# Routing of a mixture of experts: tile by tile under the output projection, in one block with the experts

## The chip, the cores and the metric

The kernel runs on one core of a Trainium2 chip. The metric is the device time of the whole program in microseconds (us); the time before is 2671.8 us, the median of three runs (2670.0 to 2675.88).

## What is computed

A trunk of two layers works on x, 1024 tokens of 1024 elements in float32. Each layer is an attention mixer with an output projection, a normalisation, a hierarchical mixture of experts, and a second normalisation:

```python
for layer in range(2):
    mix = ab_mixer(x, ...) if layer == 0 else c_mixer(x, ...)   # attention; ends with y @ w_out
    x = layer_norm(ALPHA * x + mix, ln_gain[layer, 0], ln_bias[layer, 0])
    ffn = hier_moe(x, ...)
    x = layer_norm(ALPHA * x + ffn, ln_gain[layer, 1], ln_bias[layer, 1])
```

The routing in hier_moe takes for each token the best of 4 groups by 4 group logits, and the best two of that group's 8 experts by 32 expert logits. The pairs (token, expert), 2048 of them, are then sorted by expert into blocks of 128 rows; every expert has one first block, and an expert with over 128 pairs has further ones. Each block is gathered, goes through the expert's gate, up and down matrices (1024x512, 1024x512, 512x1024), and its rows are added back with the weights of the pairs.

## The kernel before

Work is put into phases, each a block of its own with a program for every engine and a barrier at its end. For each layer: `attention`, `mixer_out`, `route`, `Moe.run`, `combine`. A float32 matrix is split in two float32r parts, a high part (ScalarE's copy, line 325 or 1574) and the rest (a subtraction, line 329, most of the time on VectorE), and a product is three matmuls in place of one.

`mixer_out` computes y @ w_out for 8 tiles of 128 tokens. Tiles 0 and 1 are computed chunk by chunk while y and w_out are being split. After that each tile is 48 matmuls of 512 columns (line 994): 24 for its first half of the columns, then the transposes of the normalised rows of the tile two before it (`router`, line 320), the other 24, and the logits of that earlier tile (`route_logits`, line 987). VectorE adds the product to the residual rows (line 1057), takes mean and variance (882 to 885); ScalarE takes the root and applies the norm (890, 902); VectorE multiplies by the gain (906); GpSimd adds the bias (910). SyncE stores the rows to DRAM, and ScalarE copies the transposed rows out of PSUM for the logits (1038), which VectorE keeps (1067). Two tiles are still to be transposed and given logits when the last product is done.

`route` starts when all logits are there. VectorE works on all 8 tiles at once in a chain of small operations (lines 1143 to 1232), each of which waits for the one before it: choice of group and experts, ranks of the pairs within their expert (TensorE adds them up, lines 1249 and 1250), number of further blocks, and one-hot rows from which TensorE makes the lists of rows of all 47 blocks (32 first blocks and up to 15 further ones; line 1253). Meanwhile SyncE loads up and down of expert 0, ScalarE splits expert 0's gate matrix and GpSimd makes its low part, and then SyncE loads the gate matrix of expert 1.

`Moe.run` clears two buffers for rows (line 1443), copies a list's column (1428), gathers rows with an indirect DMA on GpSimd (1431), and transposes them (320); ScalarE and VectorE split them, and the gate, up (1368) and down (1379) products follow. Experts are run in a loop, two in an iteration. Each of the three matrices has one raw buffer, refilled once VectorE has made its low part (1304). Results go to DRAM with an indirect DMA (1437). After 32 experts every engine reads the number of further blocks (`extra_blocks`) and runs these, if any; with these inputs there are none. SyncE fetches rows of x1 for `combine` (1272) once the last matrices have been split. `combine` then starts with loads of expert rows (1698) and adds each tile's two rows (1725, 1747, 1750) ahead of the second norm.

## Time and profile before

| | us |
|---|---|
| median of three runs | 2671.8 |
| the profiled execution's own time | 2675.71 |
| its span (first to last instruction) | 2673.9 |
| TensorE busy | 2286.0 |
| VectorE busy | 1812.6 |
| ScalarE busy | 1420.5 |
| GpSimd busy | 581.5 |

The mean granted clock of TensorE is 0.926 of full speed (2.4 GHz). Output projection and routing of the first layer lie between about 434 and 602 us of the span, those of the second between about 1795 and 1964; the experts follow to about 1222 and 2584. Times are read from the span's start; a busy time is a sum over instructions, and one of an engine which nothing waits for costs nothing.

### The profile page before, as it was taken

What the parts mean: (1) busy time and instruction counts of PE and PEld (TensorE: products, weight loads), DVE (VectorE), ACT (ScalarE), POOL (GpSimd) and SP (SyncE); (2) the same over time, 40 slices, a digit from 0 to 9 for tenths busy, and PEclk for the clock granted to TensorE, in tenths of its full rate; (3) what the DMA queues carried; (4) which work ended last, traced back from release to release, by engine and by line L of the source; (5) the groups of instructions that cost most, each with busy time, mean ns of one, the idle gap of its engine ahead of it and who ended that gap; (6) DMA issues with size and microseconds to landing.
All of it is one profiled execution on the core that took longest, in us unless ns stands there. A gap on an engine that the chain in (4) does not pass through costs nothing. (4 is left out here: it accounts for less than half of the span.)

```text
span 2673.9 us, 35450 instructions
## 1 busy us (share of the span) xinstructions
PE 2286.0 (85%) x12564; PEld 1862.1 (70%) x12564; DVE 1812.6 (68%) x2399; ACT 1420.5 (53%) x1705; POOL 581.5 (22%) x448
## 2 busy tenths in 40 slices
PE   7999997936999999992599999979649999999950
PEld 5767876835888887881478788868538888888840
DVE  3565556366888898885645455554458988889848
ACT  2454444215777777772344444442227777777732
POOL 0002332122232222322400000001212233232216
PEclk9999998958999999996699999999769999999985
DMA  3110012325999999996211111023329999999953
GB/s 111 29 29 28 29 32 82 111 110 214 369 367 367 373 369 367 372 353 231 75 42 38 39 35 43 27 66 111 145 91 366 377 379 379 372 370 360 361 221 144
DMA packets 125138, 533.52 MB, mean 200 GB/s; under 512 B 35904, under 2 KB 75864, under 8 KB 98408
## 3 DMA queue, kind: packets, MB, share of 16 engines
q1 hardware_dynamic: 102096, 496.86, 49.7%
q0 software_dynamic: 18432, 33.60, 3.4%
q10 hardware_dynamic: 4504, 1.66, 0.3%
q8 instruction: 66, 1.08, 0.2%
q14 instruction: 40, 0.33, 0.0%
HBM read 515.21 MB, written 50.39 MB: 212 GB/s over the span
## 5 line engine op out<-in xcount | busy, mean ns | idle before, releaser
L329 DVE TENSOR_TENSOR arena<-arena,arena 128x2048 fp32r<-128x2048 f32 (+1 forms) x454 | 946.4, 2119 | 98.6 <-ACT arena L1574 80.5
L1574 ACT CAST arena<-arena 128x2048 fp32r<-128x2048 f32 x380 | 705.0, 1918 | 183.6 <-PE psum L1368 103.8
L1368 PE MATMUL psum<-arena,arena 128*128 128x512 f32 x3072 | 737.2, 396 | 8.1 <-DVE arena L329 8.1
L1368 PEld LDWEIGHTS psum<-arena,arena 128*128 128x128 f32 x3072 | 571.8, 190 | 124.0 <-issue 5.6
L551 PE MATMUL psum<-arena,arena 128*128 128x512 f32 x2016 | 510.7, 405 | 5.9 <-ACT arena L659 5.8
L551 PEld LDWEIGHTS psum<-arena,arena 128*128 128x128 f32 x2016 | 375.2, 192 | 100.7 <-issue 11.6
L1379 PE MATMUL psum<-arena,arena 128*128 128x512 f32 x1536 | 367.6, 396 | 9.5 <-DVE arena L329 9.4
L1379 PEld LDWEIGHTS psum<-arena,arena 128*128 128x128 f32 x1536 | 288.4, 190 | 83.6 <-DVE arena L329 24.0
L320 PE MATMUL psum<-ident,arena 128*128 128x128 f32 x1024 | 160.4, 301 | 154.1 <-POOL arena L910 73.3
L329 DVE TENSOR_TENSOR arena<-psum,arena 128x512 fp32r<-128x512 f32 (+1 forms) x186 | 161.3, 873 | 172.8 <-ACT arena L1589 67.0
L320 PEld LDWEIGHTS psum<-ident,arena 128*128 128x128 f32 x1024 | 148.0, 198 | 181.0 <-POOL arena L910 82.9
L688 ACT ACTIVATE arena<-arena,arena 128x640 f32<-128x640 f32 (+4 forms) x192 | 120.0, 626 | 194.7 <-DVE arena L772 148.7
L1428 POOL COPY arena<-slot_rows 128x1 int32 (+1 forms) x64 | 62.9, 983 | 604.7 <-DMA expert_rows<-arena,arena 554.9
L994 PE MATMUL psum<-arena,arena 128*128 128x512 f32 x768 | 183.2, 396 | 8.1 <-ACT arena L325 6.3
L641 ACT COPY arena<-psum 128x512 f32<-128x512 f32 (+3 forms) x288 | 120.0, 466 | 129.9 <-PE psum L582 129.7
L994 PEld LDWEIGHTS psum<-arena,arena 128*128 128x128 f32 x768 | 143.6, 190 | 38.6 <-issue 6.8
L1431 POOL DMA_INDIRECT arena<-x_rows,arena x64 | 144.6, 2259 | 54.8 <-POOL arena L1428 53.1
L910 POOL TENSOR_TENSOR arena<-arena,arena 128x1024 f32<-128x1024 f32 x32 | 85.8, 2681 | 313.2 <-DVE arena L906 312.0
L582 PE MATMUL psum<-ident,arena 128*128 128x128 f32 x888 | 132.5, 280 | 23.2 <-POOL arena L876 9.2
L582 PEld LDWEIGHTS psum<-ident,arena 128*128 128x128 f32 x888 | 107.5, 143 | 52.2 <-POOL arena L876 12.1
L604 PE MATMUL psum<-arena,arena 128*64 128x128 f32 x1776 | 129.4, 287 | 0.0
L772 DVE CUSTOM_DVE_ANT_0 arena<-psum,arena 128x640 f32<-128x640 f32 (+3 forms) x192 | 104.9, 572 | 35.2 <-PE psum L570 34.5
(143 smaller groups left out, 1910.6 us busy)
## 6 DMA issues: line engine op xcount, KB each, us to landing
arena<-in_moe_w_gate SPq DMA_DIRECT2D x64, 2048.0 KB, 10.7
arena<-in_moe_w_up SPq DMA_DIRECT2D x64, 2048.0 KB, 8.6
arena<-in_moe_w_down SPq DMA_DIRECT2D x64, 2048.0 KB, 8.8
arena<-expert_rows SPq DMA_DIRECT2D x16, 1024.0 KB, 13.0
x_rows<-arena SPq DMA_DIRECT2D x24, 512.0 KB, 2.8
arena<-x_rows SPq DMA_DIRECT2D x24, 512.0 KB, 6.5
arena<-in_c_w_in SPq DMA_DIRECT2D x24, 512.0 KB, 4.1
arena<-in_x SPq DMA_DIRECT2D x16, 512.0 KB, 7.2
```

The costliest lines, as they stand in the source:

```text
L320: m = pe.transpose(dst_bank[:, j * P:(j + 1) * P], rows[:, c0 + j:rows.shape[1]:stride], ident[:])
L329: return eng.tensor_tensor(tile, src, high.bitcast(F32), ALU.subtract)
L551: mm = pe.matmul(job_bank(i, g), w[:, c * P:(c + 1) * P], xs[:, c, half_cols(g)], start=(a == 0), stop=(a == 23))
L582: mm = pe.transpose(bank(B_TURN + h)[:, (b - 4 * g) * P:(b - 4 * g + 1) * P], probs_of(s, h)[:, b * P:(b + 1) * P], ident[:])
L604: mm = pe.matmul(bank(B_OUT)[DH * h:DH * (h + 1), (t % 4) * P:(t % 4 + 1) * P], v_r[pair.kv][:, (kt + b) * P + DH * h:(kt + b) * P + DH * ...
L641: copy(probs_t[s % 2][h][:, a:b], bank(B_TURN + h)[:, 0:b - a]).then_inc(t_copied[h], 1)
L688: act.activation(probs_a[s % 2][h][:, 0:ahead + nk], biased[h][:, 0:ahead + nk], ACT.Exp, bias=low[s % 2][h], scale=-1.0, accum_out=rowsum ...
L994: return pe.matmul(bank(2 * (t % 2) + half), ys[:, c, t * P:(t + 1) * P], w[:, c, half * BANK:(half + 1) * BANK], start=(k == 0 and c == 0 ...
L1368: mm = pe.matmul(bank(o), cs[:, c * P:(c + 1) * P], ws[:, c * FF:(c + 1) * FF], start=(k == 0 and c == 0), stop=(k == 2 and c == CH - 1))
L1379: mm = pe.matmul(bank(B_Y + s), hs[:, c * P:(c + 1) * P], ws[:, c * D + s * BANK:c * D + (s + 1) * BANK], start=(k == 0 and c == 0), stop= ...
L1431: pool.indirect_dma_start(out=rows[b], out_offset=None, in_=x1_dram, in_offset=bass.IndirectOffsetOnAxis(ap=token[b], axis=0), bounds_chec ...
L1574: act.copy(w_hi[w][:, cols], self.raw[w][:, cols]).then_inc(hi_ready[w], 1)
```

## The change

`mixer_out` and `route` become a class `MixerOut`, whose parts are called from the engines' programs in `Moe.run`, so that projection, routing and experts of a layer are one block with no barrier inside. The norm is rearranged: GpSimd and ScalarE's long operation are out of it, and VectorE does subtraction of the mean with the gain, and the scaling with the bias. A tile's transposes and logits come one tile after its product in place of two. Routing is done in four groups of tiles (0 to 2, 3 to 5, 6, 7): `choose` picks experts, `ranks` (TensorE) adds up how many pairs precede, `select` makes one-hot rows, `lists` (TensorE) adds them into the lists of the first 32 blocks. The first groups are done between the norms of later tiles. What concerns further blocks is made later: `plan_extras` in the last step but one of the experts, `mark_extras` in the last, `list_extras` and `keep_extras` behind it, and all engines wait for `extras_ready` ahead of `extra_blocks`. Gain and bias are loaded after the residual rows, into the place of former weight buffers. Up and down of expert 0 are fetched when the last product is done, the low part of its gate matrix is made by VectorE after the lists are ready, and the gate matrix of expert 1 is fetched after that.

```diff
+AT_ROUTE, AT_CHOICE = 172.25, 201
+ARENA_KB = 202.75
...
+ROUTE_GROUPS = ((0, 1, 2), (3, 4, 5), (6,), (7,))
...
+                    sp.wait_ge(wl_ready, 6)
+                    for k, src in enumerate((ln_gain, ln_bias)):
+                        sp.dma_start(gain_bias[:, k, :], src[layer, 0:1, :].to_broadcast([P, D])
+                                     ).then_inc(gain_in, 16)
+                    sp.wait_ge(wl_ready, CH)
+                    moe.fetch(sp, 0, 0)
+                    for t in range(T):
+                        sp.wait_ge(normed, t + 1)
+                        sp.dma_start(x1_dram[t * P:(t + 1) * P, :], rows_all[:, t, :]).then_inc(x1_out, 16)
+                    sp.wait_ge(mix_ready, T)
...
+                    def ranks(g):
+                        pe.wait_ge(chosen_sent, g + 1)
+                        if g > 0:
+                            pe.wait_ge(added, T)
+                        for i, t in enumerate(ROUTE_GROUPS[g]):
+                            cols = rank_bank(g)[:, i * E:(i + 1) * E]
+                            mm = pe.matmul(cols, before_bf[:], chosen[:, t, :], start=True, stop=(t == 0))
+                            if t > 0:
+                                mm = pe.matmul(cols, ones_bf[:], so_far[:, t, :], start=False, stop=True)
+                        mm.then_inc(rank_ready, 1)
+                    def lists(g):
+                        for i in range(2 * len(ROUTE_GROUPS[g])):
+                            f = ENTRY[g] + i
+                            pe.wait_ge(ones_sent, f + 1)
+                            mm = pe.matmul(bank(B_LIST)[:, 0:E], at_slot[:, i, :], at_block[:, i, :],
+                                           start=(f == 0), stop=(f == ENTRIES - 1), skip_group_check=True)
+                        mm.then_inc(list_done, 1)
...
+                    for t in range(2, T):
+                        turned = 0 if t == 2 else t - 1
                         pe.wait_ge(added, t - 1)
...
+                        quarter(t, 0)
+                        if t == 3:
+                            router(1)
+                        quarter(t, 1)
+                        if t == 3:
+                            route_logits(1)
+                        router(turned)
+                        quarter(t, 2)
+                        route_logits(turned)
+                        quarter(t, 3).then_inc(mix_ready, 1)
+                        if t == 4:
+                            ranks(0)
+                        if t == 5:
+                            lists(0)
+                    ranks(1)
+                    router(T - 1)
+                    route_logits(T - 1)
+                    lists(1)
+                    ranks(2)
+                    lists(2)
+                    ranks(3)
+                    pe.wait_ge(chosen_sent, len(ROUTE_GROUPS) + 1)
+                    pe.matmul(bank(B_COUNT)[:, 0:E], ones_bf[:], so_far[:, T, :], start=True, stop=True
+                              ).then_inc(count_done, 1)
+                    lists(3)
+                    pe.wait_ge(slots_ready, 1)
...
+                    def norm(t):
+                        rows, st = rows_all[:, t, :], stats[:, t % 4, :]
                         dve.wait_ge(mix_ready, t + 1)
                         dve.wait_ge(x_in[t], 16)
                         dve.scalar_tensor_tensor(out=rows, in0=rows, scalar=ALPHA, in1=bank(2 * (t % 2), 2),
                                                  op0=ALU.mult, op1=ALU.add).then_inc(added, 1)
                         dve.wait_ge(added, t + 1)
                         norm_begin(dve, rows, t, chain, var_ready)
...
+                            dve.wait_ge(gain_in, 32)
+                        dve.scalar_tensor_tensor(out=rows, in0=rows, scalar=st[:, 12:13], in1=gain_bias[:, 0, :],
+                                                 op0=ALU.subtract, op1=ALU.mult)
+                        dve.wait_ge(root_ready, t + 1)
+                        L(dve.reciprocal(st[:, 16:17], st[:, 15:16]))
+                        dve.scalar_tensor_tensor(out=rows, in0=rows, scalar=st[:, 16:17], in1=gain_bias[:, 1, :],
+                                                 op0=ALU.mult, op1=ALU.add).then_inc(normed, 1)
...
+                    def choose(g):
...
+                        def best(values, top, candidates, first, k):
...
+                            order = down_cols[:, E - k:E]
+                            L(dve.tensor_reduce(top, values, AX.X, ALU.max))
+                            if nt == 1:
+                                L(dve.scalar_tensor_tensor(out=candidates[:, 0, :], in0=values[:, 0, :], scalar=top,
+                                                           in1=order, op0=ALU.is_equal, op1=ALU.mult))
+                            else:
+                                L(dve.tensor_tensor(candidates, values, wide(top, k), ALU.is_equal))
+                                L(dve.tensor_tensor(candidates, candidates,
+                                                    order.unsqueeze(1).to_broadcast([P, nt, k]), ALU.mult))
+                            L(dve.tensor_reduce(first, candidates, AX.X, ALU.max))
...
+                        dve.wait_ge(log_kept, t0 + nt)
+                        best(lg, gmax[:, ts], gc, gkey[:, ts], G)
+                        if nt == 1:
+                            L(dve.tensor_scalar(gn[:, 0, :], gc[:, 0, :], gkey[:, ts], NEG, ALU.is_lt, ALU.mult))
+                        else:
+                            L(dve.tensor_tensor(gn, gc, wide(gkey[:, ts], G), ALU.is_lt))
+                            L(dve.tensor_scalar(gn, gn, NEG, None, ALU.mult))
+                        for i in range(nt):
+                            ins = dve.tensor_tensor(se[:, i, :].rearrange("p (g e) -> p g e", g=G),
+                                                    logits[:, t0 + i, G:G + E].rearrange("p (g e) -> p g e", g=G),
+                                                    gn[:, i, :].unsqueeze(2).to_broadcast([P, G, PER_GROUP]), ALU.add)
+                        L(ins)
+                        ones = [one[:, f0 + k * nt:f0 + (k + 1) * nt, :] for k in range(2)]
+                        for k, top in enumerate((m1[:, ts], m2[:, ts])):
+                            first = key[:, f0 + k * nt:f0 + (k + 1) * nt]
+                            best(se, top, ca, first, E)
+                            if nt == 1:
+                                L(dve.tensor_scalar(ones[k][:, 0, :], ca[:, 0, :], first, None, ALU.is_equal))
+                            else:
+                                L(dve.tensor_tensor(ones[k], ca, wide(first, E), ALU.is_equal))
+                            if k == 0:
+                                L(dve.scalar_tensor_tensor(out=se, in0=ones[0], scalar=2 * NEG, in1=se,
+                                                           op0=ALU.mult, op1=ALU.add))
+                        ins = dve.tensor_tensor(chosen[:, ts, :], ones[0], ones[1], ALU.add)
+                        for t in group[:-1]:
+                            L(ins)
+                            ins = dve.tensor_tensor(so_far[:, t + 1, :], so_far[:, t, :], chosen[:, t, :], ALU.add)
+                        ins.then_inc(chosen_sent, 1)
+                        dve.wait_ge(chosen_sent, g + 1)
+                        t = group[-1]
+                        ins = dve.tensor_tensor(so_far[:, t + 1, :], so_far[:, t, :], chosen[:, t, :], ALU.add)
+                        if g == len(ROUTE_GROUPS) - 1:
+                            ins.then_inc(chosen_sent, 1)
+                        else:
+                            L(ins)
...
+                    def select(g):
...
+                        w = work[:, 0:2 * nt * E]
+                        L(dve.tensor_tensor(w.rearrange("p (k m) -> p k m", k=2),
+                                            one[:, fs, :].rearrange("p (k t) e -> p k (t e)", k=2),
+                                            rank_bank(g)[:, 0:nt * E].unsqueeze(1).to_broadcast([P, 2, nt * E]),
+                                            ALU.mult))
+                        L(dve.tensor_reduce(rank[:, fs], w.rearrange("p (f e) -> p f e", e=E), AX.X, ALU.add))
+                        if g > 0:
+                            dve.wait_ge(list_done, g)
+                        for i in range(2 * nt):
+                            f = f0 + i
+                            dve.tensor_scalar(at_slot[:, i, :], iota_cols[:], rank[:, f:f + 1], None, ALU.is_equal)
+                            dve.tensor_scalar(at_block[:, i, :], down_cols[:], key[:, f:f + 1], pair_id[:, f:f + 1],
+                                              ALU.is_equal, ALU.mult).then_inc(ones_sent, 1)
+                    norm(0)
+                    norm(1)
+                    keep_logits(0)
+                    norm(2)
+                    L(dve.memset(so_far[:, 0, :], 0.0))
+                    keep_logits(1)
+                    keep_logits(2)
+                    norm(3)
+                    choose(0)
+                    keep_logits(3)
+                    norm(4)
+                    select(0)
+                    keep_logits(4)
+                    norm(5)
+                    keep_logits(5)
+                    norm(6)
+                    choose(1)
+                    keep_logits(6)
+                    norm(7)
+                    select(1)
+                    choose(2)
+                    keep_logits(7)
+                    choose(3)
+                    select(2)
+                    select(3)
...
+                    dve.wait_ge(list_done, len(ROUTE_GROUPS))
+                    L(dve.tensor_scalar(empty, bank(B_LIST)[:, 0:E], 0.0, float(NO_ROW), ALU.is_equal, ALU.mult))
+                    L(dve.scalar_tensor_tensor(out=listed, in0=bank(B_LIST)[:, 0:E], scalar=-1.0, in1=empty,
+                                               op0=ALU.add, op1=ALU.add))
+                    L(dve.tensor_copy(slot_rows[:, 0:E, 1], listed))
+                    dve.tensor_scalar(slot_rows[:, 0:E, 0], slot_rows[:, 0:E, 1], 1, None, ALU.arith_shift_right
+                                      ).then_inc(slots_ready, 1)
...
+                def mark_extras(dve):
+                    chain = Chain(dve, chain_sem, dve_links[0])
+                    L = chain.link
+                    L(dve.tensor_scalar(blk, rank, float(P), None, ALU.is_ge))
...
+                                        col.unsqueeze(2).to_broadcast([P, ENTRIES, EXTRA]), ALU.is_equal))
+                    dve.tensor_tensor(at_block_x, at_block_x,
+                                      pair_id[:].unsqueeze(2).to_broadcast([P, ENTRIES, EXTRA]), ALU.mult)
+                    dve.tensor_tensor(at_slot_x, iota_cols[:].unsqueeze(1).to_broadcast([P, ENTRIES, P]),
+                                      rank_in.unsqueeze(2).to_broadcast([P, ENTRIES, P]), ALU.is_equal
+                                      ).then_inc(extra_sent, 1)
+                    dve_links[0] += chain.n
...
+                def keep_extras(dve):
+                    chain = Chain(dve, chain_sem, dve_links[0])
+                    L = chain.link
+                    dve.wait_ge(extra_done, 1)
...
+                                      ALU.arith_shift_right).then_inc(extras_ready, 1)
...
+                    sp.wait_ge(before.extras_ready, 1)
                     count = extra_blocks(sp, more)
...
+                    before.gpsimd(pool)
                     for b in range(2):
                         ins = pool.memset(rows[b], 0.0)
                     ins.then_inc(rows_ready, 1)
+                    pool.wait_ge(before.x1_out, 16 * TILES)
+                    pool.wait_ge(before.slots_ready, 1)
...
+                    before.list_extras(pe)
...
+                    before.scalar(act)
+                    split(GATE, 0)
                     split(UP, 0)
+                    before.exponentials(act)
+                    act.wait_ge(before.x1_out, 16 * TILES)
                     act.wait_ge(xt_ready, 1 + 1)
...
+                    before.vector(dve)
+                    dve.wait_ge(before.x1_out, 16 * TILES)
+                    split(GATE, 0)
                     split(UP, 0)
+                    before.pair_weights(dve)
...
+                        elif not last:
+                            before.plan_extras(dve)
+                        else:
+                            before.mark_extras(dve)
                         dve.wait_ge(down_done, 1 + e + 1)
...
+                    before.keep_extras(dve)
                     dve.wait_ge(y_out[0], 8 * EXPERTS)
                     extra_blocks(dve, more)
...
-            phase(mixer_out, layer, moe)
-            phase(route, layer, moe)
-            phase(moe.run)
+            phase(lambda: moe.run(MixerOut(layer, moe)))
```

## Rows read from the trace of the kernel before

**Rows 1.** Busy time by stage: routing and experts of layer 0; from:to, length, engines, granted clock, DMA share, GB/s.
```profile
559.00:601.00 42.00, 7.67 (x34) 7.03 (x34) 39.09 (x133) 5.31 (x5) 9.14 (x2) 0.50 0.39 150
...
622.00:1242.00 620.00, 581.65 (x2680) 476.13 (x2679) 518.46 (x319) 448.24 (x331) 160.60 (x122) 0.98 0.90 345
```

**Rows 2.** Timeline of the projection, layer 0: start us, duration us, engine, line, operation, idle before.
```profile
467.18 1.16 PE L320 MATMUL psum<-ident,arena 128*128 128x128 f32 x8 [1.76 <-POOL arena L910]
...
487.50 1.22 DVE L1057 SCALAR_TENSOR_TENSOR arena<-arena,psum 128x1024 f32<-128x1024 f32 x1 [7.39 <-PE psum L994]
...
489.00 5.74 PE L994 MATMUL psum<-arena,arena 128*128 128x512 f32 x24
...
501.14 1.22 DVE L1057 SCALAR_TENSOR_TENSOR arena<-arena,psum 128x1024 f32<-128x1024 f32 x1 [7.39 <-PE psum L994]
```

**Rows 3.** Timeline after the last product of the projection, layer 0.
```profile
542.06 1.22 DVE L1057 SCALAR_TENSOR_TENSOR arena<-arena,psum 128x1024 f32<-128x1024 f32 x1 [7.40 <-PE psum L994]
...
544.88 0.15 DVE L885 TENSOR_SCALAR stats<-stats 128x1 f32<-128x1 f32 x1
...
551.85 1.95 PE L320 MATMUL psum<-ident,arena 128*128 128x128 f32 x8
...
558.57 0.20 DVE L1067 TENSOR_TENSOR logits<-psum,b_route 128x36 f32<-128x36 f32 x1 [6.29 <-PE psum L987]
```

**Rows 4.** Timeline of the routing, layer 0.
```profile
562.74 9.14 POOL L329 TENSOR_TENSOR arena<-arena,arena 128x2048 fp32r<-128x2048 f32 x2 [12.11 <-ACT arena L1242]
562.89 4.63 DVE L1138 TENSOR_TENSOR arena<-arena,down_cols 128x256 f32<-128x256 f32 x1
...
573.57 0.43 DVE L1138 TENSOR_TENSOR arena<-arena,down_cols 128x256 f32<-128x256 f32 x1
...
579.53 1.32 DVE L1188 SCALAR_TENSOR_TENSOR arena<-arena 128x32 f32<-128x32 f32 x6
...
591.12 7.07 PE L1253 MATMUL psum<-arena 128*128 128x47 f32 x32 [14.73 <-DVE arena L1213]
...
598.51 0.65 DVE L1220 TENSOR_REDUCE arena<-arena 128x15 f32<-128x480 f32 x1
...
600.96 0.19 DVE L1232 COPY slot_rows<-arena 128x47 int32<-128x47 int32 x1
```

**Rows 5.** Timeline of the start of the experts, layer 0.
```profile
603.66 4.49 DVE L329 TENSOR_TENSOR arena<-arena,arena 128x2048 fp32r<-128x2048 f32 x2 [2.50 <-ACT arena L1574]
...
606.98 2.27 POOL L1431 DMA_INDIRECT arena<-x_rows,arena  x1 [0.99 <-POOL arena L1428]
608.40 0.36 SPq L1304 DMA_DIRECT2D arena<-in_moe_w_up  x1
...
617.21 1.95 PE L320 MATMUL psum<-ident,arena 128*128 128x128 f32 x8 [19.03 <-DMA arena<-x_rows,arena]
...
620.24 1.23 DVE L329 TENSOR_TENSOR arena<-psum,arena 128x1024 fp32r<-128x1024 f32 x1 [12.09 <-ACT arena L1578]
...
621.61 7.89 PE L1368 MATMUL psum<-arena,arena 128*128 128x512 f32 x24 [2.45 <-DVE arena L329]
```

**Rows 6.** DMA issues from 620 to 622 us: the third gather, count, us to landing.
```profile
arena<-x_rows,arena POOLq DMA_INDIRECT x1, 4.2
```

**Rows 7.** The same stretch in layer 1: line 1057's first and last start, and the timeline.
```profile
L1057 DVE SCALAR_TENSOR_TENSOR arena<-arena,psum x16: 1214/1222/1222, 458.4 to 1904.0; 128x1024 f32<-128x1024 f32 x16
```
```profile
1983.80 7.77 PE L1368 MATMUL psum<-arena,arena 128*128 128x512 f32 x24 [2.45 <-DVE arena L329]
```

**Rows 8.** Timeline of the end of the experts and the start of combine, layer 0.
```profile
1210.72 1.75 SPq L1272 DMA_DIRECT2D arena<-x_rows  x4
...
1212.64 7.66 PE L1379 MATMUL psum<-arena,arena 128*128 128x512 f32 x24 [1.40 <-DVE arena L329]
...
1221.98 0.98 POOL L1437 DMA_INDIRECT expert_rows<-arena,arena  x1 [14.68 <-DVE arena L1659]
1232.30 0.32 SPq L1698 DMA_DIRECT2D arena<-expert_rows  x1
```

**Rows 9.** DMA issues from 1220 to 1224 us: the last scatter, count, us to landing.
```profile
expert_rows<-arena,arena POOLq DMA_INDIRECT x1, 3.7
```

551 lines of the change are left out of this document (242 added, 309 removed).

## The prediction, made before the changed kernel ran

> **What bounds the kernel now.** I read the busy time by stage first. Between the output projection and the experts lie 42 us in which TensorE works 7.67 us and VectorE 39.09 us, and the DMAs move 150 GB/s: a chain on VectorE sets the end there, nothing else [rows 1]. In the expert stage TensorE is busy 581.65 of 620 us with the DMA engines at 0.90, so that stage runs near two limits and the routing near none. Then the timeline. In the projection TensorE is the bound: tiles follow each other every 501.14 - 487.50 = 13.64 us, and 2 x 5.74 = 11.5 of them are the product [rows 2]; 2.2 are transposes and logits. VectorE waits 7.4 us of each such period. From the sum behind the last product, at 542.06 [rows 3], to the first matmul of an expert, at 621.61 [rows 5], 79.6 us go by; in the second layer it is 1983.80 - 1904.0 = 79.8 us [rows 7]. The change works on these two stretches and on the end of the experts, so I rebuild each stretch from its durations, in the clock of layer 0, and take the difference.
>
> **The projection.** VectorE's idle 7.4 us of each period take up the routing of tiles 0 to 2 and 3 to 5: choose for three tiles is 24 operations of 32 to 96 elements at 0.22 us for 32 (1.32 / 6) and some 0.29 for 96, about 6.2 us, and select for three tiles about 3.5 us [rows 4]. The norm on VectorE costs 2.97 us up to the variance (542.06 to 545.03) and then two operations like the 1.22 us ones and a reciprocal, 5.7 us in all [rows 3]; 5.7 + 6.2 + 0.2 for the logits is 12.1 of 13.64 us, so it fits, by 1.5 us. If it did not, each overrun would hold up the transposes. A tile's transposes stand 24 matmuls (5.74 us) behind its product and need the norm after 5.7 us and two handovers: 0.2 us late in each of five tiles, 1.0 us. More of the routing's TensorE work now comes before the last product's end: one tile's transposes and logits (2.2) and one more tile's logits (1.5), the ranks of the first group (0.5) and its lists, 6 of 16 entries of which all took 7.07 us at the 0.50 clock [rows 1, 4], at full clock 1.4. The stall of 1.76 us at the first transposes goes [rows 2]. Sum: 1.0 + 2.2 + 1.5 + 0.5 + 1.4 - 1.8 = +4.8, so the last product ends at 546.9. Bounds: +3 (all hidden between weight loads) and +9 (each group's wait costs TensorE a micro-stop). The gain and bias now come behind 4 MB of residual rows; I cost that at nothing, as the first tile's transposes come 5.7 us after its sum; were they late, it would be up to 3 us.
>
> **From the last product to the lists.** The last tile's norm ends 5.8 us later. Transposes, copy and logits of that tile took 558.57 - 551.85 = 6.72 us at the low clock [rows 3], which I keep: TensorE has had nothing to do for 5 us. They end at +12.5. VectorE meanwhile does select(1), 3.3 us, and choose(2), 16 chained operations at 0.22 or 3.5 us [rows 4]: +12.6, level with it. Then one after another: keep the logits 0.2, choose(3) 3.7, select(2) 1.25 (two small operations, two entries of 0.4), TensorE's lists(2) and ranks(3) with handovers 1.5, select(3) 1.25, lists(3) 0.6, the count 0.2, four closing operations 0.9. Sum 22.2 us, so the lists are ready at 569.1 against 601.15 [rows 4]. Bounds: 20.5, if the lists overlap with VectorE, and 27, if every handover costs as much again. What goes besides is GpSimd's low part of the gate matrix, beside which one VectorE operation took 4.63 us where its twin took 0.43 [rows 4].
>
> **From the lists to the first expert.** Before: 20.5 us (601.15 to 621.61), with a barrier, the clearing of two buffers, and a gather whose generation on GpSimd took 2.27 us and which landed 10.2 us after its start, at 617.2 [rows 5]. Barrier and clearing go from the path. VectorE however now has two matrices to split here, each 4.49 us [rows 5], where it had one: 0.45 + 9.0 + 1.3 for the pair weights, then the 1.23 us for the columns: +12.1 is the floor. The gather: 1.2 to 4 us for copy and generation, 3.2 us (4.2 - 1.0, the third gather, no load beside it) [rows 6] to 7.9 us (10.2 - 2.27, beside a weight load issued at 608.40) for its landing, and 4.4 for transposes, copy and columns: +9 to +16. The next weight load is issued 4.5 us after the lists, when the first gather is mostly through. I take +14, nearer to the row with the load: first matmul at 583.1. That is 38.5 us earlier per layer, 77 for both.
>
> The trace shows VectorE and GpSimd holding each other up (4.63 against 0.43 us) [rows 4]. The Trainium skill, "SBUF — State Buffer", section "SBUF: two separate sides", says that these two share one pair of ports which the one that starts first holds for its whole instruction. That speaks against this piece of the change: GpSimd's copy and generation fall among VectorE's four half splits. By that rule the value is +14, without it +12.1.
>
> **The end of the experts.** plan_extras (about 4.2 us) stands where no gate split is left, and ends with the down product at its side. mark_extras is some 17 operations, the largest over 2048, 512 and 480 elements, 2.3 (half of 4.49), 0.7 and 0.65 us [rows 4, 5]: 6.9 us, beside the last down product of 7.66 us [rows 8]; hidden, by 0.7 us. list_extras is not: 16 entries at 7.07 us [rows 4] begin when that product ends (1220.3) and end at 1227.4, then 0.9 us of VectorE: 1228.4. Before, all that was left was the last scatter, 1221.98 plus 3.7 us to its landing or 1225.7 [rows 8, 9], and the jump out to the next phase's first load at 1232.30 [rows 8]. So +2.7 us, if that jump costs what it did. SyncE too waits for these lists, and its four loads of x1 rows (2 MB), which went out at 1210.72 [rows 8], go out at about 1229.7 to 1231.4, just ahead of the first expert rows. At 345 GB/s [rows 1] they are 6.1 us of transfer, of which 3.3 to 5 have gone by when the first load of combine is issued at 1235.0. I take 2.3 for what is left; bounds 0 and 6. Behind that combine goes at the pace of its vector work and gives nothing back. Together 5.0 us a layer; bounds 1 and 8.
>
> The Trainium skill, "DMA: Bandwidth & Descriptors", section "Queues, rings and completion order", says that each DMA engine takes a ring's descriptors in their order. If so, combine's first rows stand wholly behind the x1 rows issued on the same queue, and the 2.3 us are due; if the loads shared the engines freely the first rows would be later still, by sharing with 2 MB, not less.
>
> **Sum.** Per layer 38.5 - 5.0 = 33.5 us, twice 67. The profiled execution took 2675.7 us, 3.9 above the median of 2671.8, so the forecast is 2608.7 by its own time and **2605** by the median. Its own range comes from the bounds: 2587 (+3, 20.5, 12.1 and 1) to 2631 (+9, 27, 16 and 8).
>
> **Rivals.**
> - *The weights set the start of the experts.* The gate matrix of expert 1 was loaded under the routing, and is now issued 4.5 us after the lists, with up of expert 1 right behind: 2 x 2 MB, 11.6 us at 345 GB/s [rows 1]. If the stage is bound by its bytes, the gain behind the lists is lost to them, 11.6 us a layer: 2605 + 23 = 2628. For it: DMA share 0.90. Against: TensorE was busy 94% of that stage, and both loads land before the first gate product (7.9 us) and the up product behind it need them.
> - *VectorE becomes the bound of the projection.* If small operations with broadcasts cost 0.4 us rather than 0.22 to 0.29, choose(0) and choose(1) overrun the 1.5 us of slack by some 3 us each, choose(2) and (3) by 2.5 each behind it: 11 us a layer, 2627. Against: such operations with 256 elements took 0.43 us [rows 4].
> - *The expert loop falls into a slower rhythm: slower than before.* It starts with other distances between gathers and weight loads; VectorE (518 of 620 us), GpSimd's generation and the DMA engines are so full [rows 1] that a gather that always comes late would delay every expert. It decides from 33.5 / 32 = 1.05 us per expert; at 1.5 us, 96 for 64 experts, the time is 2605 + 96 = 2701. Against: in both layers the same rhythm came about, and a gather is issued more than an expert ahead.
> - *The late lists cost more than thought.* If the jump out of the block waits for cold code or the x1 rows fully (8 to 12 us a layer more than 5), 2621 to 2629.
>
> **How the numbers follow.** Forecast with its own range 0.67; weights 0.09; VectorE 0.08; late lists 0.10; slower rhythm 0.04; the change not doing what it says (routing left serial by some wait) 0.02, near 2665. Time 2605; the range 2586 to 2631 takes in the first four. About 0.2% (5 us) is what a measurement of this kernel can tell. Faster 0.94, within it 0.02, slower 0.04.
>
> **What would show it.** Right, in the first layer: the last tile's sum at about 547, the lists' closing cast at 569, the first gate product at 583, TensorE with no more than some 0.3 us of waiting per tile in the projection, and an expert stage of 620 us, within 3; at its end the first load of combine 14 to 15 us after the last down product in place of 12. Wrong: TensorE waiting in the projection for a VectorE that is full; waits for weights in the first experts; another period of the expert loop, which would make every other step small; or a longer pause between the lists of further blocks and combine.

## The result, and the profile after

The changed kernel takes 2603.3 us (median of four runs, 2598.5 to 2609.6) against 2672.7 for the kernel before on the same chip: ratio 0.974, 95% interval 0.972 to 0.976, so 2.6% faster. The forecast was 2605, with a range of 2586 to 2631. One execution of the repeat below (4711 us) and one of the kernel before beside it (4328) were in a slow state and enter no number. The profiled execution took 2601.8 us, its span is 2599.6. The table splits the 74.3 us between the two spans (2673.9 - 2599.6) at places found in both traces; L0 and L1 are the two layers.

| from, to | before L0, L1 | after L0, L1 | difference |
|---|---|---|---|
| start to layer 0's first output sum | 458.4 | 452.7 | -5.7 |
| first to last output sum | 83.7, 83.7 | 89.2, 89.0 | +5.5, +5.3 |
| last sum to lists of first blocks | 59.1, 59.1 | 21.6, 21.6 | -37.5, -37.5 |
| lists to first expert product | 20.5, 20.7 | 11.75, 21.66 | -8.7, +0.9 |
| first product to end of last down product | 598.7, 598.5 | 601.1, 598.8 | +2.4, +0.3 |
| last down product to combine's first load | 12.0, 11.7 | 11.9, 11.3 | -0.1, -0.4 |
| combine and layer 1's attention; last combine | 588.0, 80.0 | 589.2, 79.9 | +1.1, -0.1 |

The same stretches by busy time (columns as in [rows 1]): projection, its end to the lists, experts of layer 0. In the middle one VectorE is still the busiest, but the stretch is 21.5 us, half of the 42 us of [rows 1].

```profile
453.00:542.00 89.00, 87.53 (x474) 73.75 (x473) 51.99 (x127) 8.43 (x14) 0.09 (x1) 1.00 0.18 71
542.00:563.50 21.50, 10.71 (x55) 9.89 (x55) 18.40 (x73) 9.79 (x7) 1.75 (x2) 0.58 0.56 221
576.00:1176.00 600.00, 582.12 (x2680) 475.36 (x2679) 524.88 (x345) 445.96 (x329) 160.29 (x121) 0.99 0.92 351
```

The projection's timeline answers to [rows 2 and 3]. A period is now 541.89 - 527.80 = 14.09 us; TensorE waits 0.21 us for VectorE's norm before the transposes, and VectorE, which runs a whole choose inside the period, still idles 2.6 us before the next sum.

```profile
527.80 1.22 DVE L1167 SCALAR_TENSOR_TENSOR arena<-arena,psum 128x1024 f32<-128x1024 f32 x1 [2.65 <-PE psum L1060]
...
533.41 1.15 PE L327 MATMUL psum<-ident,arena 128*128 128x128 f32 x8 [0.21 <-DVE arena L1177]
...
537.14 1.87 PE L1032 MATMUL psum<-w_route,arena 128*128 128x36 f32 x16
...
541.89 1.22 DVE L1167 SCALAR_TENSOR_TENSOR arena<-arena,psum 128x1024 f32<-128x1024 f32 x1 [2.58 <-PE psum L1060]
```

Behind the last sum: the last tile's transposes at +5.6 us, its logits kept at +12.4, one choosing, two selects and two list passes, and the closing cast at 563.34, where [rows 4] had 600.96.

```profile
547.50 1.97 PE L327 MATMUL psum<-ident,arena 128*128 128x128 f32 x8 [3.94 <-DVE arena L1177]
...
554.33 0.19 DVE L1182 TENSOR_TENSOR logits<-psum,b_route 128x36 f32<-128x36 f32 x1
...
559.28 1.06 PE L1053 MATMUL psum<-arena,arena 128*128 128x32 f32 x4 [2.47 <-DVE arena L1261]
...
563.34 0.18 DVE L1298 TENSOR_SCALAR slot_rows<-slot_rows 128x32 int32<-128x32 int32 x1
```

The start of the experts answers to [rows 5]. Layer 0:

```profile
563.66 0.20 POOL L1550 COPY arena<-slot_rows 128x1 int32<-128x1 int32 x1 [19.91 <-DVE slot_rows L1298]
563.73 8.89 DVE L336 TENSOR_TENSOR arena<-arena,arena 128x2048 fp32r<-128x2048 f32 x4
564.86 2.26 POOL L1553 DMA_INDIRECT arena<-x_rows,arena  x1 [0.99 <-POOL arena L1550]
...
568.25 0.33 SPq L1418 DMA_DIRECT2D arena<-in_moe_w_gate  x1
...
570.62 1.94 PE L327 MATMUL psum<-ident,arena 128*128 128x128 f32 x8 [8.06 <-DMA arena<-x_rows,arena]
...
573.90 1.22 DVE L336 TENSOR_TENSOR arena<-psum,arena 128x1024 fp32r<-128x1024 f32 x1
```

Layer 1, the same instructions:

```profile
1888.21 8.89 DVE L336 TENSOR_TENSOR arena<-arena,arena 128x2048 fp32r<-128x2048 f32 x4
...
1888.45 2.09 POOL L1550 COPY arena<-slot_rows 128x1 int32<-128x1 int32 x1 [20.22 <-DVE slot_rows L1298]
1891.48 2.19 POOL L1553 DMA_INDIRECT arena<-x_rows,arena  x1 [0.94 <-POOL arena L1550]
...
1892.73 0.33 SPq L1418 DMA_DIRECT2D arena<-in_moe_w_gate  x1
...
1905.14 1.95 PE L327 MATMUL psum<-ident,arena 128*128 128x128 f32 x8 [18.10 <-DMA arena<-x_rows,arena]
...
1909.66 7.93 PE L1483 MATMUL psum<-arena,arena 128*128 128x512 f32 x24 [2.58 <-DVE arena L336]
```

The order of the first two rows is what matters. In layer 0 GpSimd's copy of one column starts 0.07 us before VectorE's split and takes 0.20 us; in layer 1 it starts 0.24 us after it and takes 2.09. Counted from the lists, the gather is then generated 2.1 us later, its descriptors are complete only at 1893.67, behind the weight load issued at 1892.73, and its rows come 11.5 us after that; in layer 0 they came 3.5 us after, with the load issued 1.1 us behind them. A race of 0.3 us decides over some 10 us. The kernel before had the long case in both layers: there the copy took 2.2 us, the load went out 0.7 to 0.8 us ahead of the complete descriptors, and the first transposes came 8.0 and 8.4 us behind them; layer 1 kept this and gained nothing in this stretch.

The end of layer 0's experts answers to [rows 8]: the lists of further blocks take 3.64 us, not the 7.07 of [rows 4]. TensorE comes out of a down product, and the granted clock is 1.00 here, where it was 0.50 in the routing [rows 1]. VectorE's last operation on them ends at 1180.66, before the last scatter has landed (issued at 1178.02, landed 3.2 us later, so at 1181.2).

```profile
1167.97 8.37 PE L1494 MATMUL psum<-arena,arena 128*128 128x512 f32 x24 [1.40 <-DVE arena L336]
1176.18 3.64 PE L1119 MATMUL psum<-arena,arena 128*128 128x15 f32 x32
...
1178.02 0.98 POOL L1559 DMA_INDIRECT expert_rows<-arena,arena  x1 [12.80 <-DVE arena L1801]
...
1180.49 0.17 DVE L1370 TENSOR_SCALAR slot_rows<-slot_rows 128x15 int32<-128x15 int32 x1
1181.92 2.49 SPq L1386 DMA_DIRECT2D arena<-x_rows  x4
1188.25 0.32 SPq L1841 DMA_DIRECT2D arena<-expert_rows  x1
```

The stretch from 1176 to 1180 us (columns as in [rows 1]), and the last scatter in the view of DMA issues:

```profile
1176.00:1180.00 4.00, 3.82 (x34) 3.69 (x32) 0.83 (x2) 0.59 (x1) 0.98 (x1) 1.00 0.11 44
```
```profile
expert_rows<-arena,arena POOLq DMA_INDIRECT x1, 3.2
```

### The profile page after: what moved, and what is told of

It reads as the page before. It is cut to its first block and busy times, and to the rows that moved or that the text cites. A ratio compares the mean times of both kernels' runs of the same rounds, so it can differ in the third digit from the quotient of the medians.

```text
span 2599.6 us, 35642 instructions
## 1 busy us (share of the span) xinstructions
PE 2287.6 (88%) x12656; PEld 1859.9 (72%) x12656; DVE 1836.2 (71%) x2475; ACT 1400.2 (54%) x1689; POOL 529.7 (20%) x434
## 5 line engine op out<-in xcount | busy, mean ns | idle before, releaser
L1703 ACT CAST arena<-arena 128x2048 fp32r<-128x2048 f32 x384 | 712.3, 1917 | 150.2 <-PE psum L1483 85.6
L1494 PE MATMUL psum<-arena,arena 128*128 128x512 f32 x1536 | 369.2, 396 | 10.2 <-DVE arena L336 10.2
L1553 POOL DMA_INDIRECT arena<-x_rows,arena x64 | 137.7, 2152 | 54.7 <-POOL arena L1550 47.1
L579 PE MATMUL psum<-arena,arena 64*128 64x320 f32 (+5 forms) x1056 | 115.8, 339 | 7.9 <-DVE arena L781 6.7
```

What stands on the lines that cost most here:

```text
L1494: mm = pe.matmul(bank(B_Y + s), hs[:, c * P:(c + 1) * P], ws[:, c * D + s * BANK:c * D + (s + 1) * BANK], start=(k == 0 and c == 0), stop= ...
L1553: pool.indirect_dma_start(out=rows[b], out_offset=None, in_=x1_dram, in_offset=bass.IndirectOffsetOnAxis(ap=token[b], axis=0), bounds_chec ...
L1703: act.copy(w_hi[w][:, cols], self.raw[w][:, cols]).then_inc(hi_ready[w], 1)
```

## The experiments

Each differs from the changed kernel (2603.3) by the edit shown. The kernel before took 2673.8 to 2675.9 beside them and 2672.7 beside the changed kernel, so totals of different groups can be compared to about 3 us. Stretches are those of one profile each.

**The same kernel again.**

> The changed kernel once more, for its spread. Its first profile shows two things that the prediction did not have: the second layer needs 21.7 us from its lists to its first expert product where the first needs 11.8, and attention of layer 0 ended 5.7 us earlier than before the change. Theory A (who takes the port first is chance): from run to run either layer can have either value, 11.8 or about 21. Theory B (something fixed in layer 1): again 11.8 and 21.7. Attention: if its 5.7 us are chance, the projection of layer 0 starts anywhere between 428 and 435 us again; if the change brought them, at 429 within 0.5. Time 2603, within 6.

2601.6 us (2599.4 to 2604.0), ratio 0.973 (0.971 to 0.975). Lists to first product: 11.76 and 20.40, and the first sum at 452.7 us again. This is Theory B: the difference between the layers is no accident of one run. In all six traces in which nothing decides the race (the changed kernel twice, load_late, after_product, router_after and no_extra_lists) the copy is ahead of the split in layer 0 and behind it in layer 1. What is fixed in layer 1 stays open. First to last sum was 90.5 us in layer 0 this time (88.9 in layer 1), so that stretch too can be 1.3 us longer by itself.

**Who sets the start of the experts.** Three edits move one thing each.

```diff
copy_first:
                     dve.wait_ge(before.x1_out, 16 * TILES)
+                    dve.wait_ge(tokens_ready, 1 + 1)
                     split(GATE, 0)
copy_behind:
                     pool.wait_ge(rows_ready, 1 + 1)
+                    pool.wait_ge(lo_ready[GATE], 1 + 1)
load_late:
                     sp.wait_ge(lo_ready[GATE], 1 + 2)
+                    sp.wait_ge(rows_in[0], 16)
                     self.fetch(sp, 1, GATE)
```

> VectorE waits for GpSimd's first token copy ahead of the gate split; so the copy never stands behind it, but the generation of the gather's descriptors, 1 us later, still does. Theory A: both layers as layer 0 was, 11.5 to 12.5 us from lists to first product, time 2593 to 2598. Rival B (load contention alone makes the 21.7 us): no change in layer 1, time 2603.

> GpSimd waits, ahead of its first token copy, until VectorE has made the first half of the low part of the gate matrix, so its copy always stands behind running splits. Theory A (VectorE's split in progress holds up GpSimd's copy and descriptor generation, and the weight load then goes out ahead of the gather): both layers need 20 to 23 us from the lists to the first expert product; the time is some 10 us above a run in which one layer was lucky, 2610 to 2615. Rival B (the long case comes of something else in layer 1): layer 0 is late by the 2.3 us of the wait alone, 14 us, and the time rises by 2 to 5 us.

> SyncE holds back the load of expert 1's gate matrix until the first gather has landed; the order of copy and split is left to chance. If the gather's long landing (11.5 us from its generation in layer 1) comes of the 2 MB load that went out beside it, layer 1 needs about 13 to 14 us from lists to first product even where its copy was held up, and the time is 2594 to 2598. If it comes of descriptor generation being blocked by VectorE alone, layer 1 stays near 21 us. Price of the later load: none in either case, as the gate product of expert 1 comes over 20 us later.

| kernel | total us | ratio (interval) | lists to first product, L0, L1 |
|---|---|---|---|
| changed | 2603.3 | 0.974 (0.972 to 0.976) | 11.75, 21.66 |
| copy_first | 2594.5 | 0.970 (0.968 to 0.972) | 12.02, 12.22 |
| copy_behind | 2613.9 | 0.978 (0.976 to 0.979) | 20.45, 20.48 |
| load_late | 2599.7 | 0.973 (0.971 to 0.974) | 11.72, 13.74 |

Both layers can be given either value by the order of a 0.2 us copy and a split: copy_first and copy_behind are Theory A, in stretch and total. copy_behind gets to its 20.5 us on a slightly different way: its wait ends the gather's generation 2.2 to 2.3 us later still than in layer 1 of the changed kernel, and the transposes come 7.9 and 8.1 us after it, where those took 11.5. Timeline of copy_first, layer 1: the copy is alone, VectorE waits 0.44 us for it, and the gather's descriptors are out (1893.72 + 2.42) 1.25 us ahead of the load.

```profile
1892.59 0.18 POOL L1550 COPY arena<-slot_rows 128x1 int32<-128x1 int32 x1 [20.23 <-DVE slot_rows L1298]
1892.87 8.90 DVE L336 TENSOR_TENSOR arena<-arena,arena 128x2048 fp32r<-128x2048 f32 x4 [0.44 <-POOL arena L1550]
1893.72 2.42 POOL L1553 DMA_INDIRECT arena<-x_rows,arena  x1 [0.94 <-POOL arena L1550]
...
1897.39 0.33 SPq L1418 DMA_DIRECT2D arena<-in_moe_w_gate  x1
```

load_late takes the second half by itself. In its layer 1 the copy is still behind the split (2.09 us), but no load goes ahead of the gather, whose rows come 3.5 us after its descriptors (1888.32 + 2.20 to 1894.02):

```profile
1885.29 2.09 POOL L1551 COPY arena<-slot_rows 128x1 int32<-128x1 int32 x1 [20.23 <-DVE slot_rows L1298]
1888.32 2.20 POOL L1554 DMA_INDIRECT arena<-x_rows,arena  x1 [0.94 <-POOL arena L1551]
...
1893.86 0.33 SPq L1418 DMA_DIRECT2D arena<-in_moe_w_gate  x1
1894.05 1.95 PE L327 MATMUL psum<-ident,arena 128*128 128x128 f32 x8 [10.17 <-DMA arena<-x_rows,arena]
```

So of layer 1's 9.4 us over copy_first about 1.5 are the late copy and 8 the load in front of the gather. That is read from the stretch of one trace; the median total fell by 3.6 us only, and missed the expected 2594 to 2598 by 1.7.

**The gather made first, and the columns kept earlier.**

```diff
                     dve.wait_ge(before.x1_out, 16 * TILES)
+                    dve.wait_ge(tokens_ready, 1 + 2)
                     split(GATE, 0)
+                    keep_cols(0, 0)
                     split(UP, 0)
                     before.pair_weights(dve)
-                    keep_cols(0, 0)
```

> VectorE waits, before it splits expert 0's gate weights, until GpSimd has copied the second block's token numbers, which comes behind the making of the first gather; and it keeps block 0's columns before it splits the up weights. Theory A (the first gather's place against VectorE's split and against the load of the next gate weights sets the start): the copy takes 0.20 us and the making of the first gather 1.0 us instead of 2.1 and 2.2, the rows land 3.3 us behind it, the turn (1.95), ScalarE's copy (1.01) and keep_cols (1.23) follow, so from the lists to the first expert product about 10.4 us in both layers (the changed kernel: 11.75 and 21.66; with only the copy put first: 12.02 and 12.22), total about 2590 (2586 to 2594). Rival B (the up weights' split, now later, is late for expert 0's up product, or the split is the limit whatever the order): 12 us or more from lists to first product, or PE idle 2 us or more within expert 0, total as with the copy first alone, 2594 or above.

2589.9 us, ratio 0.969 (0.967 to 0.971); lists to first product 10.40 and 10.58 us. Theory A to 0.2 us: what sets the start now is the chain of GpSimd's copy, the gather's generation and landing, the transposes, ScalarE's copy and VectorE's columns, and nothing is lost behind it. With VectorE held back the generation takes 1.10 us in layer 1 (1.23 in layer 0). The edit makes two changes at once; by the traces 1.3 of the 1.6 us under copy_first in layer 1 come of the shorter generation (2.42 to 1.10), and the earlier columns are left with 0.3.

```profile
1885.68 0.18 POOL L1550 COPY arena<-slot_rows 128x1 int32<-128x1 int32 x1 [20.23 <-DVE slot_rows L1298]
...
1886.81 1.10 POOL L1553 DMA_INDIRECT arena<-x_rows,arena  x1 [0.94 <-POOL arena L1550]
...
1888.20 4.49 DVE L336 TENSOR_TENSOR arena<-arena,arena 128x2048 fp32r<-128x2048 f32 x2 [2.68 <-POOL arena L1550]
```

**What the overlap is worth.** In after_product the choosing of groups 0 and 1 comes behind the last product; in router_after all turns and logits do too, with the new norm kept.

```diff
after_product (TensorE; VectorE's choose and select likewise):
-                        if t == 4:
-                            ranks(0)
-                        if t == 5:
-                            lists(0)
-                    ranks(1)
                     router(T - 1)
                     route_logits(T - 1)
+                    ranks(0)
+                    lists(0)
+                    ranks(1)
                     lists(1)
router_after (TensorE; ScalarE's copies and VectorE's keep_logits likewise):
-                        router(turned)
-                        route_logits(turned)
...
+                    for t in range(T):
+                        router(t)
+                        route_logits(t)
```

> Only the place of the choosing is changed: groups 0 and 1 of the tokens are chosen, selected, ranked and listed after the last output product and not under the projection. Theory A (the prediction's: VectorE does this inside the projection's idle time, so that it costs nothing there): first to last sum stays at 89 us (within 1), last sum to lists rises from 21.6 by two choosings of 5.7 us and their selects and ranks, 12 to 15 us, in each layer; total 2602 plus 24 to 30, about 2629. Rival B (the +5.3 us in the projection are the price of this work): first to last sum falls to 84 to 86, total only 14 to 20 us longer, about 2619. Rival C (the overlap brings nothing, the whole gain came from doing the tail's work in one pass): total 2602 to 2606.

> The new norm, all on VectorE, stays as in the changed kernel, but every router pass (turn of the tile, ScalarE's copy, logits) comes after the last output product, and so all of the choosing, ranking and listing too. Theory A (the 5.3 us that the projection is longer are TensorE's router passes for seven tiles and 1 us of choosing): first to last sum falls from 89.0 to 83.7 to 85 us; last sum to lists rises from 21.6 to 55 to 62 us (the kernel before had 59.1 with lists of all blocks in it); about 33 us a layer longer, total 2660 to 2675. Rival B (the norm on VectorE alone is the price, a tile's norm there being late for the next tile's first product): first to last sum stays at 88 us or more, total 2668 to 2680.

| kernel | total us | first to last sum | last sum to lists |
|---|---|---|---|
| changed | 2603.3 | 89.2, 89.0 | 21.6, 21.6 |
| after_product | 2634.2 (ratio 0.984, 0.982 to 0.987) | 88.0, 88.1 | 37.9, 37.9 |
| router_after | 2652.0 (ratio 0.991, 0.990 to 0.993) | 66.9, 66.9 | 66.3, 66.1 |

after_product: choosing, selecting and listing of groups 0 and 1 cost 1.0 us under the projection and 16.3 behind it, 15.3 a layer and 31 in all; Theory A, its sum a little low. router_after fell outside both theories, which took the kernel before's 83.7 us for the products alone, though turns and logits of six tiles lie in it. Without them a period is 525.37 - 514.48 = 10.89 us, so each router pass (a tile's transposes and logits) costs 14.09 - 10.89 = 3.20 us at the full clock, the 0.21 us of waiting included (and two of them stand in tile 3's period). Behind the products, at the low clock (0.50 from 531.8 to 544.8 us) and with nothing to fill its 1.10 us of waiting, a pass takes 538.36 - 531.87 = 6.49:

```profile
531.87 1.95 PE L327 MATMUL psum<-ident,arena 128*128 128x128 f32 x8
534.92 3.63 PE L1032 MATMUL psum<-w_route,arena 128*128 128x36 f32 x16 [1.10 <-ACT arena L1127]
538.36 1.95 PE L327 MATMUL psum<-ident,arena 128*128 128x128 f32 x8
```

**What the late lists are worth.** In no_extra_lists marks, lists and keeping of further blocks are left out altogether (these inputs have none), and a memset in their place says that they are ready; in lists_early they are made in the routing again.

```diff
no_extra_lists:
                 def list_extras(pe):
-                    for f in range(ENTRIES):
...
+                    pass
...
+                    dve.memset(one_line, 1.0).then_inc(extras_ready, 1)
lists_early:
                     L(dve.tensor_copy(count_row, bank(B_COUNT)[:, 0:E]))
+                    plan_extras(dve)
+                    mark_extras(dve)
...
                     lists(3)
+                    list_extras(pe)
```

> The marks, the lists and the keeping of the blocks beyond the first are left out (the plan is still made, so the blocks beyond the first work on no lists). Theory A (the prediction's step: the 32 passes of list_extras lie between the last down product and the combine and cost 2.7 to 5 us a layer): total 5 to 10 us less, 2592 to 2598, and last down product to first combine load falls from 11.9 to 7 to 9 us. Rival B (the passes take 3.7 us at the full clock and end before the last scatter has landed, and so cost nothing): within 1.5 us a layer of the changed kernel, 2600 to 2604, last down product to combine load 11.3 to 12.0 us.

2598.3 us, ratio 0.972 (0.970 to 0.974). Last down product to combine's first load: 12.4 and 11.5 us, so not shorter without the lists than with them (11.9 and 11.3): Rival B. The total is 5.0 us lower, below Rival B's range and at the edge of Theory A's, and 3.1 of it are in layer 1's start (18.52 us from lists to first product against 21.66, with the copy, the split and the load in the same order), so by its total alone this run would not tell the rivals apart; the stretch does.

> Only the deferral is undone: the marks, the 32 list passes and the keeping of the blocks beyond the first are made in the routing, before the experts. Theory A (its worth is VectorE's marks, some 7 us, and the passes at the lower clock, 7.07 us as in the kernel before, both on the way to the first gather): last sum to first product rises by 14 to 20 us a layer, total 2630 to 2642. Rival B (the passes take 3.7 us as at the end of the experts in the changed kernel, and the marks lie beside the turn and the gather): 5 to 9 us a layer, total 2612 to 2620.

2626.1 us, ratio 0.982 (0.980 to 0.984). The lists of first blocks come 10.2 us later (31.9 after the last sum, by VectorE's marks), and the passes, at the low clock (0.50 from 574 to 581 us), take 7.01 us again and hold TensorE and then VectorE's split:

```profile
574.10 7.01 PE L1120 MATMUL psum<-arena,arena 128*128 128x15 f32 x32 [10.46 <-DVE arena L1363]
...
574.95 0.20 POOL L1558 COPY arena<-slot_rows 128x1 int32<-128x1 int32 x1 [30.14 <-DVE slot_rows L1304]
```

From last sum to first product this is 50.4 us in both layers, against 33.4 and 43.3: +17.0 and +7.1. Layer 0 is Theory A; in layer 1 the held-back split lets GpSimd go first, and 10 us of the loss come back. That is why the total missed Theory A's range from below.

**The kernel before, for the place of its stages.**

> The kernel before once more, for the place of its stages. Theory A (the time up to layer 0's first output sum differs between builds but is the same in every run of one build): first sum at 458.4 us as in the first profile of the kernel before, within 0.3. Rival B (it differs from run to run): anywhere from 452.7 to 460.7, as the other kernels have it.

One execution, 2676.4 us. First sum at 455.9 us, against 458.4 in its first profile: Rival B, as it was put, since one build differs by 2.5 us from run to run. The two profiles of the changed kernel agree (452.7), and builds that differ from it only behind this stage have 452.7 to 460.7; two profiles of a build are too few to say how much of this is the build. Up to this sum the trace says nothing for or against a change of less than 8 us.

**A version that beats both.** gen_first, and in combine the norm as the projection has it: GpSimd's product and sum and ScalarE's apply are left out, VectorE does both in two operations.

```diff
...
-                        norm_scale(dve, t - 1, chain, root_ready, scale_ready)
...
+                        chain.link(dve.reciprocal(st[:, 16:17], st[:, 15:16]))
+                        dve.scalar_tensor_tensor(out=x1_tiles[t - 1], in0=x1_tiles[t - 1], scalar=st[:, 16:17],
+                                                 in1=gain_bias[:, 1, :], op0=ALU.mult, op1=ALU.add
+                                                 ).then_inc(shifted, 1)
...
+                        dve.scalar_tensor_tensor(out=rows, in0=rows, scalar=stats[:, t % 4, 12:13],
+                                                 in1=gain_bias[:, 0, :], op0=ALU.subtract, op1=ALU.mult)
```

> As gen_first, and the combine's norm is written as the projection's norm is in the changed kernel: gain and bias applied by VectorE, GpSimd's product with the gain and ScalarE's apply left out. Theory A (the combine's tile period of some 8.3 us is set by VectorE and GpSimd taking turns): the last layer's combine falls from 79.9 to about 68, total 11 to 15 us under gen_first (about 2577). Rival B (the period is set by its loads, stores or the additions): under 3 us from gen_first, 2587 to 2590.

2562.5 us, ratio 0.958 (0.957 to 0.960): 27.4 us under gen_first and 40.8 under the changed kernel. The mechanism is Theory A's; its size was put at half, because only one combine was counted: 8 tiles of two layers by 8.32 - 6.67 us are 26.4. The last combine alone fell from 79.8 to 64.4 us, where 68 was expected. A combine period of gen_first, with GpSimd at VectorE's side, and the same operations of gen_first_combine:

```profile
2540.30 2.34 POOL L915 TENSOR_TENSOR arena<-arena,arena 128x1024 f32<-128x1024 f32 x1 [2.70 <-ACT arena L911]
...
2540.49 3.23 DVE L1891 SCALAR_TENSOR_TENSOR arena<-arena,w_pair 128x1024 f32<-128x1024 f32 x1
...
2548.81 3.23 DVE L1891 SCALAR_TENSOR_TENSOR arena<-arena,w_pair 128x1024 f32<-128x1024 f32 x1
```

```profile
2519.29 1.28 DVE L1883 SCALAR_TENSOR_TENSOR arena<-arena,w_pair 128x1024 f32<-128x1024 f32 x1
...
2525.96 1.28 DVE L1883 SCALAR_TENSOR_TENSOR arena<-arena,w_pair 128x1024 f32<-128x1024 f32 x1
```

VectorE has two more long operations per tile and its period still falls from 8.32 to 6.67 us, because the first addition takes 1.28 us alone and 3.23 beside GpSimd (the second 1.23 and 3.24). VectorE is the bound in both, busy 39.3 and 39.2 of 40 us of the last combine (columns as in [rows 1]; gen_first, then gen_first_combine):

```profile
2530.00:2570.00 40.00, 0.00 (x0) 0.00 (x0) 39.31 (x41) 10.94 (x14) 26.82 (x10) 0.50 0.21 87
```
```profile
2510.00:2550.00 40.00, 0.00 (x0) 0.00 (x0) 39.16 (x55) 5.37 (x10) 0.00 (x0) 0.50 0.41 170
```

## Why the prediction was right, and where not

- *The bound.* Right: the gain came from the two stretches it named. The stretches that it summed (first to last sum, sum to lists, lists to product, last product to combine) are worth 72.3 us in the two profiles, against its 67. Experts and attention took 3.8 of it back, and the 5.7 us before the first sum, which no term of it covers, came on top.
- *The projection, +4.8.* Measured +5.5 and +5.3 (+6.8 in layer 0 of the repeat). The cover it named held: 1.0 us for the choosing of two groups (after_product), 0.21 us of waiting per tile. Its price of 2.2 us for a tile's transposes and logits was too low: it took 2 x 5.74 us as the product, but a period with nothing but the product is 10.89 us in router_after, which leaves 2.75 of the 13.64 in the kernel before and 3.20 in the changed one.
- *Last product to lists, 22.2.* Measured 21.6. after_product shows what the overlap takes off this stretch: 16.3 us.
- *Lists to first product, 14.* The step that failed, though its mean over both layers (16.7) hides it. The 12.1 called the floor was the sum of VectorE's work in the order written; layer 0 ran there (11.75), and gen_first shows that it was the floor of an order, not of the work: 10.4. The 16 called the ceiling was 5.7 too low: layer 1 took 21.66. Its two sources, VectorE in GpSimd's way and a load in the gather's, were both named, but as a surcharge to be averaged, and with the load going out when the gather was mostly through; in fact they act in a chain, in which the load comes first only where VectorE made the gather late. copy_first and copy_behind show it, load_late parts them (1.5 and 8 us).
- *The end of the experts, +5.0.* Failed on a size: the 32 passes were priced at 7.07 us, from a row at clock 0.50; they ran at the full clock in 3.64, under the last scatter. Measured -0.1 and -0.4, and no_extra_lists shows no cost in the stretch. Of its own signs this one failed: the first load of combine came 11.9 us after the last down product, where 14 to 15 were to show it right. The term of 2.3 us for the x1 rows was not due in layer 0 of the profiled execution, where combine's first operation follows its first load after 4.78 us, as before (4.92); but it was 7.32 in layer 0 of the repeat, 7.08 in copy_behind and 6.61 in after_product, where the last x1 rows landed 2.8 to 3.4 us behind that load's issue, against 1.8. So the term is real in some executions. Together the stretch gave back 10.5 us, and the start of the experts took 5.4 more than forecast: two errors of opposite sign, hidden by each other in the total.
- *Luck.* 2605 against 2603.3 is closer than the terms are: besides these two errors, the 3.8 us of experts and attention and the 5.7 before the first sum were in no term, and each is larger than the miss of 1.7. What does not lean on luck is the main term, from the last sum to the lists: 36.9 us a layer forecast, 37.5 measured.
- *Sums.* The bounds of the single terms (+3, 20.5, 12.1, 1 and +9, 27, 16, 8) add up to 2586 and 2633, not 2587 and 2631. Two loads of 2 MB are 12.2 us at 345 GB/s by the working that makes one 6.1, not 11.6. The measured time lies inside the range either way.
- *Rivals.* Weights: at 598.8 to 601.1 us of experts (before 598.5 to 598.7) no loss of 11.6 a layer, but in layer 1 one load of theirs did delay the start. VectorE the bound of the projection: no, it idles 2.6 us in a period that holds a whole choose. Slower rhythm: +2.4 and +0.3 us in 32 experts, no. Late lists: no, 11.9 and 11.3 us to combine's first load, before 12.0 and 11.7.

The forecast's remark that VectorE and GpSimd hold each other up has its proof here: the first column's copy takes 0.18 to 0.21 us ahead of the split and 2.06 to 2.09 behind it, in all traces of the changed kernel and its variants. The Trainium skill, "SBUF — State Buffer", section "SBUF: two separate sides", says that the two share ports which the one that starts first keeps for its whole instruction; the trace agrees, and the copy ends (1888.45 + 2.09 = 1890.54) with the first of the split's four operations (1888.21 + 8.89 / 4 = 1890.43).

## What to carry to other kernels

Take the price of a moved TensorE step at the clock of the place it is moved to: the list passes took 3.64 us right behind a product and 7.01 in a pause, a router pass 3.20 and 6.49 (part of that waiting). Where two engines are released by one event and one of them starts the critical DMA, say which goes first by a wait: a 0.3 us race was worth up to 10 us a layer here, and the wait cost 0.44. Read a change by its stretches, since errors and shifts of unrelated stages (8 us up to the first sum) are as large as single steps.

## What was not expected of the hardware

- GpSimd's copy starts 0.32 us after the list's cast began in layer 0 and 0.63 us after it in layer 1, in all traces but two: copy_behind, which holds it back, and gen_first_combine, where layer 1 has 0.32 too. The 0.63 also stands in gen_first, where no VectorE split is beside it. Why is open.
- An indirect gather whose descriptors are complete 1 to 3 us after a 2 MB load was issued has its transposes 7.9 (copy_behind, layer 0) to 11.5 us later, against 3.4 to 3.7 us when the load follows it (4.6 in lists_early, whose rows landed after 3.2). With the same order and the load 0.95 us ahead it was 8.3 us in no_extra_lists and 11.5 in the changed kernel; what makes that spread is open.
- The time up to the first sum of layer 0 differs by up to 8 us between builds whose instructions there stand in the same order, and by 2.5 us between two runs of one build. Not explained.
